# HGRN scan of a hybrid trunk step: half-width score levels, summed before the output product, with the finest levels scaled on GpSimd

## The reference

```
b = jnp.cumsum(logf.astype(jnp.float32), axis=2)
causal = jnp.tril(jnp.ones((C, C), dtype=bool))[:, :, None, None]
diff = b[:, :, :, None] - b[:, :, None, :]
decay = jnp.exp(jnp.where(causal, diff, -jnp.inf))
attn = jnp.einsum('bnthk,bnshk,bntshk->bnhts', q, k, decay)
o_intra = jnp.einsum('bnhts,bnshv->bnthv', attn, v)
b_last = b[:, :, -1]
ds = jnp.einsum('bnshk,bnshv->bnhkv', k * jnp.exp(b_last[:, :, None] - b), v)
...
return S * dec[..., None] + dS, S
...
o_inter = jnp.einsum('bnthk,bnhkv->bnthv', q * jnp.exp(b), jnp.moveaxis(S_start, 0, 1))
return (o_intra + o_inter).reshape(B, T, H, V), S_fin
```

## Time and profile before

| | |
|---|---|
| median of 3 runs | 3807.51 us (3803.77 to 3820.35) |
| profiled execution, its own time | 3803.54 us |
| its span | 3801.8 us |
| PE busy | 3068.4 us (81%) |
| DVE busy | 1796.5 us (47%) |
| ACT busy | 764.6 us (20%) |
| POOL busy | 809.9 us (21%) |
| 386 to 419 us: PE, DVE, ACT, POOL busy | 29.53, 24.94, 10.08, 0.00 of 33.00 us |
| granted clock of PE from 352 to 616 us | 1.00 |

### The profile page before, as it was taken

The page is one execution under the profiler, slowest core; times in us unless marked ns, Lnnn a source line. Parts: engine busy times, 40 slices in busy tenths (PEclk is TensorE's granted clock), DMA queues, the critical chain, the costliest instruction groups (busy, mean ns, idle before and its releaser), DMA issues. The chain is left out here.

```text
span 3801.8 us, 41834 instructions
## 1 busy us (share of the span) xinstructions
PE 3068.4 (81%) x15224; PEld 1731.3 (46%) x15224; DVE 1796.5 (47%) x3832; ACT 764.6 (20%) x1538; POOL 809.9 (21%) x812
## 2 busy tenths in 40 slices
PE   8698886689699999979987776777777777777776
PEld 2475775247476666747543323233323333333332
DVE  0004776424444333333145676556566655664443
ACT  0202223100322121221021212112212121221212
POOL 0000000000000001000014443444444443443442
PEclk9899999699799999989998888888888888988888
DMA  6211000111010110115149998999999999999996
GB/s 268 96 43 43 20 20 12 54 59 58 26 38 29 38 37 29 38 44 193 50 161 356 380 377 327 389 379 375 365 394 382 379 371 383 382 382 378 375 376 252
DMA packets 123662, 794.63 MB, mean 209 GB/s; under 512 B 15127, under 2 KB 16919, under 8 KB 39032
## 3 DMA queue, kind: packets, MB, share of 16 engines
q0 software_dynamic: 92160, 671.13, 44.7%
q1 hardware_dynamic: 31352, 121.42, 9.0%
HBM read 775.98 MB, written 16.52 MB: 208 GB/s over the span
## 5 line engine op out<-in xcount | busy, mean ns | idle before, releaser
L1997 PE MATMUL pr_psy<-pr_rows,pr_diag 128*128 128x512 f32 x2560 | 1312.0, 673 | 447.9 <-ACT pr_diag L2052 447.6
L1997 PEld LDWEIGHTS pr_psy<-pr_rows,pr_diag 128*128 128x128 f32 x2560 | 541.5, 217 | 1215.4 <-issue 665.3
L2179 DVE CUSTOM_DVE_ANT_0 pr_rows<-pr_rows,pr_h_tok 128x1024 f32<-128x1024 f32 x640 | 779.6, 1226 | 647.2 <-DMA pr_rows<-in_p_uv,pr_now 644.9
L1935 POOL DMA_INDIRECT pr_rows<-in_p_uv,pr_now x640 | 727.7, 1137 | 1031.2 <-PE pr_psy L1997 909.0
L1547 POOL TENSOR_TENSOR yT<-rw_sys,rw_bmask 128x128 f32<-128x128 f32 x40 | 18.1, 454 | 1543.6 <-DVE rw_sys L1646 1543.6
L2047 ACT ACTIVATE pr_act<-pr_dot 128x4 f32<-128x4 f32 x160 | 32.8, 205 | 1326.8 <-DVEq L2183 1326.8
L1291 PE MATMUL rw_gate_ps<-hT,rw_gate_w 128*128 128x320 f32 x768 | 262.8, 461 | 3.2 <-ACT rw_gate L1485 3.2
L2052 ACT ACTIVATE pr_diag<-con,pr_weight 128x128 f32<-128x128 f32 x640 | 204.6, 390 | 58.2 <-DVE pr_weight L2189 57.4
L1291 PEld LDWEIGHTS rw_gate_ps<-hT,rw_gate_w 128*128 128x128 f32 x768 | 129.4, 190 | 55.1 <-issue 14.4
L287 PE MATMUL hg_ps<-hT,hg_w 128*128 128x320 f32 x512 | 139.9, 437 | 16.4 <-DMA hg_w<-in_w_in 16.4
L287 PE MATMUL rw_ps<-hT,rw_w 128*128 128x320 f32 x480 | 131.5, 438 | 12.7 <-DMA rw_w<-in_w_in 12.7
(11 more groups left out here) (372 smaller groups left out, 3255.7 us busy)
## 6 DMA issues: line engine op xcount, KB each, us to landing
ada_w<-in_w_ada SPq DMA_DIRECT2D x8, 3072.0 KB, 10.5
rw_gate_w<-in_w_in SPq DMA_DIRECT2D x24, 512.0 KB, 4.1
pr_rows<-in_p_uv,pr_now POOLq DMA_INDIRECT x640, 9.3
hg_w<-in_w_in SPq DMA_DIRECT2D x16, 512.0 KB, 3.4
rw_w<-in_w_in SPq DMA_DIRECT2D x15, 512.0 KB, 3.5
gate_scratch<-rw_gate SPq DMA_DIRECT2D x24, 320.0 KB, 4.2
mg_gate<-gate_scratch SPq DMA_DIRECT2D x24, 320.0 KB, 3.3
mg_wb<-in_w_branch SPq DMA_DIRECT2D x24, 256.0 KB, 2.7
```

Source lines behind the costliest of these rows:

```text
L1935: nc.gpsimd.indirect_dma_start(out=rows[:, r].rearrange("p u d -> p (u d)"), out_offset=None, in_=A["p_uv"], in_offset=bass.IndirectOffset ...
L1997: last = nc.tensor.matmul(ps_y[:, c % 2, a], diag[:, r], rows[:, r, 1, a * 512:(a + 1) * 512], start=(first and r == 0), stop=False, skip_ ...
L2179: nc.vector.tensor_tensor_reduce(out=rows[:, r, 0], in0=rows[:, r, 0], in1=h_tok[:, c], scale=1.0, scalar=0.0, op0=ALU.mult, op1=ALU.add, ...
```

## The change

Levels 1 to 6 and the diagonal only connect positions of the same half of a chunk (64 positions). Their products are now done for each half alone, into the two halves of the partitions, so that each takes 64 columns of a PSUM bank. Level 0 connects one half with the other, and takes 64 columns as well (`FAR`). The eight arrays of a step, 1024 columns before, are 512 now (`HG_W`). VectorE multiplies them with a mask of that form, waits for itself, and sums the seven arrays of the halves into `near` with one reduce. The output then needs one product for each half (`near`), one for `FAR`, and the product with the state in two halves.

The scaling of levels 4 to 6 and of the two end arrays is now done by GpSimd in a list of its own, after `exp_done` of the second exponential; its last instruction raises `x_ready`. VectorE keeps levels 0 to 3, spread over steps 3 and 4, and raises `scaled`. TensorE waits for both before the transposes. `ps_s` and `ps_o` share one tensor of four banks.

```diff
--- before.py
+++ after.py
@@ -37,6 +37,9 @@
 GN_EPS = 64e-5
 LEVELS = [64, 32, 16, 8, 4, 2, 1]
 NL = len(LEVELS)
+H64 = [slice(0, HD), slice(HD, P)]
+HG_W = (NL + 1) * HD
+FAR = slice(NL * HD, HG_W)
 
 
 PARAMS = [("b_ada", 48), ("norm1", 8), ("norm2", 8), ("final", 8), ("lb", 8), ("hgrn_norm", 1),
@@ -365,20 +368,21 @@
                         nc.vector.tensor_copy(i_tok[:, c], ps_i[:, c % 2]).then_inc(i_taken, 1)
 
         NE = NL + 2
-        mask = sb("mask", [P, 2, NL + 1, P])
+        mask = sb("mask", [P, 2, HG_W])
         reset = sb("reset", [P, RESET_W])
         lf = sb("lf", [P, RESET_W])
         cum = sb("cum", [P, RESET_W])
         kT = sb("k", [P, 2, NCH, P])
         E = sb("E", [P, 2, NE, NCH, P])
         dec = sb("dec", [P, 2, NCH])
-        att = sb("att", [P, 2, NL + 1, P])
+        att = sb("att", [P, 2, HG_W])
+        near = sb("near", [P, 2, HD])
         khat = sb("khat", [P, 2, NCH, P])
         S = sb("S", [P, 3, DK])
         S_in = sb("S_in", [P, 8, DK])
-        ps_s = ctx.enter_context(nc.psum_tensor("hg_pss", [P, 2, NL + 1, P], F32))
+        ps_so = ctx.enter_context(nc.psum_tensor("hg_pss", [P, 4, 512], F32))
+        ps_s, ps_o = ps_so[:, 0:2], ps_so[:, 2:4, 0:HD]
         ps_t = ctx.enter_context(nc.psum_tensor("hg_pst", [P, 1024], F32))
-        ps_o = ctx.enter_context(nc.psum_tensor("hg_pso", [P, 512], F32))
 
         ps_d = ps_t[:, 6 * P:7 * P]
         ps_y = ctx.enter_context(nc.psum_tensor("hg_psy", [P, 512], F32))
...
@@ -397,6 +402,19 @@
 
 
         steps = [(g, g // 4, g % 4, c) for g in range(8) for c in order(g // 4)]
+        POOL_FROM = 4
+
+        def scale_level(eng, g, v):
+
+            d, h, b, w = g // 4, g % 4, g % 2, LEVELS[v]
+            q = qT[:, h].rearrange("p (c t) -> p c t", t=P)
+            lo, hi = (kT[:, b], q) if d == 0 else (q, kT[:, b])
+            x = E[:, b, v].rearrange("p c (n t) -> p c n t", t=2 * w)
+            for src, s in ((lo, slice(0, w)), (hi, slice(w, 2 * w))):
+                y = src.rearrange("p c (n t) -> p c n t", t=2 * w)[:, :, :, s]
+                ins = eng.tensor_tensor(x[:, :, :, s], x[:, :, :, s], y, ALU.mult)
+            return ins
+
         with nc.Block() as block:
             @block.sync
             def _(sp):
@@ -448,6 +466,17 @@
                 for n in range(18, 20):
                     take_hyena(n)
 
+            @block.gpsimd
+            def _(pool):
+                for g in range(8):
+                    pool.wait_ge(exp_done, 2 * g + 2)
+                    q = qT[:, g % 4].rearrange("p (c t) -> p c t", t=P)
+                    for v in range(POOL_FROM, NL):
+                        scale_level(nc.gpsimd, g, v)
+                    for n, x in ((NL, q), (NL + 1, kT[:, g % 2])):
+                        ins = nc.gpsimd.tensor_tensor(E[:, g % 2, n], E[:, g % 2, n], x, ALU.mult)
+                    ins.then_inc(x_ready, 1)
+
             @block.tensor
             def _(pe):
                 def hyena(n, first, end):
@@ -474,6 +503,7 @@
                     b = g % 2
                     if n % NCH == 0:
                         pe.wait_ge(x_ready, g + 1)
+                        pe.wait_ge(scaled, g + 1)
                         if g >= 1:
                             pe.wait_ge(khat_ready, g)
                         for cc in range(NCH):
@@ -481,9 +511,13 @@
                         last.then_inc(tr_done, 1)
                     if n >= 2:
                         pe.wait_ge(att_ready, n - 1)
-                    for v in range(NL):
-                        nc.tensor.matmul(ps_s[:, n % 2, v], E[:, b, v, c], E[:, b, v, c], start=True, stop=True)
-                    nc.tensor.matmul(ps_s[:, n % 2, NL], kT[:, b, c], qT[:, h, c * P:(c + 1) * P],
+                    q = qT[:, h, c * P:(c + 1) * P]
+                    for v in range(1, NL + 1):
+                        lhs, rhs = (E[:, b, v, c], E[:, b, v, c]) if v < NL else (kT[:, b, c], q)
+                        for half in H64:
+                            nc.tensor.matmul(ps_s[half, n % 2, (v - 1) * HD:v * HD], lhs[:, half], rhs[:, half],
+                                             start=True, stop=True)
+                    nc.tensor.matmul(ps_s[:, n % 2, FAR], E[:, b, 0, c], E[:, b, 0, c, H64[1 - d]],
                                      start=True, stop=True).then_inc(s_done, 1)
 
                 def outputs(n):
@@ -505,9 +539,9 @@
                     if n >= 1:
                         pe.wait_ge(o_taken, n)
                     first = n % NCH == 0
-                    for v in range(NL + 1):
-                        last = nc.tensor.matmul(ps_o[:, 0:P], iv, att[:, n % 2, v], start=(v == 0),
-                                                stop=(v == NL and first))
+                    for i, half in enumerate(H64):
+                        nc.tensor.matmul(ps_o[:, i], iv[half], near[half, n % 2], start=True, stop=first and i == d)
+                    last = nc.tensor.matmul(ps_o[:, 1 - d], iv, att[:, n % 2, FAR], start=False, stop=first)
                     if not first:
                         k = n % NCH
                         if k == 1:
@@ -516,7 +550,8 @@
                         else:
                             pe.wait_ge(st_ready, 4 * g + k)
                             src = S[:, 1 + k % 2]
-                        last = nc.tensor.matmul(ps_o[:, 0:P], src, E[:, b, NL, c], start=False, stop=True)
+                        for i, half in enumerate(H64):
+                            last = nc.tensor.matmul(ps_o[:, i], src, E[:, b, NL, c, half], start=False, stop=True)
                     last.then_inc(o_done, 1)
 
                 for n in range(4):
...
@@ -583,29 +616,24 @@
                             nc.vector.tensor_tensor(E[:, b, NL + 1], exc, zero, ALU.subtract).then_inc(dec_sub, 1)
 
                     def scale(v):
-                        w = LEVELS[v]
-                        dve.wait_ge(exp_done, 2 * g + (1 if v < 4 else 2))
-                        x = E[:, b, v].rearrange("p c (n t) -> p c n t", t=2 * w)
-                        for src, s in ((lo, slice(0, w)), (hi, slice(w, 2 * w))):
-                            y = src.rearrange("p c (n t) -> p c n t", t=2 * w)[:, :, :, s]
-                            nc.vector.tensor_tensor(x[:, :, :, s], x[:, :, :, s], y, ALU.mult)
-
-                    def scale_ends():
-                        nc.vector.tensor_tensor(E[:, b, NL], E[:, b, NL], q, ALU.mult)
-                        nc.vector.tensor_tensor(E[:, b, NL + 1], E[:, b, NL + 1], kT[:, b], ALU.mult).then_inc(
-                            x_ready, 1)
+                        dve.wait_ge(exp_done, 2 * g + 1)
+                        ins = scale_level(nc.vector, g, v)
+                        if v == POOL_FROM - 1:
+                            ins.then_inc(scaled, 1)
 
                     return [[gates], [sums] + [lambda v=v: level(v) for v in range(4)],
                             [lambda v=v: level(v) for v in range(4, NL)] + [to_ends],
-                            [lambda v=v: scale(v) for v in range(4)],
-                            [lambda v=v: scale(v) for v in range(4, NL)] + [scale_ends]]
+                            [lambda v=v: scale(v) for v in range(2)],
+                            [lambda v=v: scale(v) for v in range(2, POOL_FROM)]]
 
                 def chunk(n, meanwhile):
                     g, d, h, c = steps[n]
                     dve.wait_ge(s_done, n + 1)
                     if n >= 2:
                         dve.wait_ge(o_done, n - 1)
-                    nc.vector.tensor_tensor(att[:, n % 2], ps_s[:, n % 2], mask[:, d], ALU.mult).then_inc(att_ready, 1)
+                    link(nc.vector.tensor_tensor(att[:, n % 2], ps_s[:, n % 2], mask[:, d], ALU.mult))
+                    nc.vector.tensor_reduce(near[:, n % 2], att[:, n % 2, 0:NL * HD].rearrange("p (v t) -> p t v", t=HD),
+                                            AX, ALU.add).then_inc(att_ready, 1)
                     k = n % NCH
                     if k != NCH - 1:
                         dve.wait_ge(ds_done, 4 * g + k + 1)
@@ -627,11 +655,11 @@
                     for step in meanwhile:
                         step()
                     dve.wait_ge(o_done, n + 1)
-                    o = K.yT[0][:, h, c * P:(c + 1) * P]
+                    o = K.yT[0][:, h, c * P:(c + 1) * P].rearrange("p (i t) -> p i t", i=2)
                     if d == 0:
-                        nc.vector.tensor_copy(o, ps_o[:, 0:P]).then_inc(o_taken, 1)
+                        nc.vector.tensor_copy(o, ps_o).then_inc(o_taken, 1)
                     else:
-                        nc.vector.tensor_tensor(o, o, ps_o[:, 0:P], ALU.add).then_inc(o_taken, 1)
+                        nc.vector.tensor_tensor(o, o, ps_o, ALU.add).then_inc(o_taken, 1)
 
                 for steps_of in prepare(0):
                     for step in steps_of:
...
@@ -2295,12 +2322,15 @@
         con[:, CCOL["tneg"] + 1 + c] = -tl[c * P:(c + 1) * P]
```

(13 more changed lines are left out.)

## The result

The changed kernel took 3838.4 us (median of six runs, 3831.2 to 3841.6) and the one before, on the same chip, 3814.9 us (3803.8 to 3824.6). The ratio is 1.0059, 95% interval 1.0039 to 1.0078: slower by 23.5 us between the medians and by 22.5 us by the ratio, where +23.0 was predicted. (The predicted time itself, about 3831, came from an earlier median of 3807.5 for the kernel before, 7 us lower than here.) The profiled execution of the changed kernel took 3837.5 us, its span 3835.7 us. Medians of the kernel before moved between 3814.0 and 3817.1 over the four sets of runs here. A length read from the traces leaves out what the other stages do, and I use two.

The account below looks back on a forecast made before the run. A ring of waits through TensorE, VectorE and ScalarE was taken to bound the HGRN scan's rounds 0 to 6. Seven handovers at +3.9 us (+27.3) and round 7 (-4.3) gave +23.0 on 3807.5: about 3831 us, range 3808 to 3847.

Parts of the forecast that it names:

- L518's records: Sign in the new profile: TensorE's half products of the scores would stand 0.043 us apart.
- To the end of the second exp: From a round's start: 26.28 less 2 x 0.23 (scores) and 0.59 (wait), plus 2 x 0.15 (mask product and sum): 25.5 us.
- GpSimd's chain: Eight GpSimd instructions between second exp and transposes: 8.05 us, plus 1.9 while VectorE's products with two SBUF inputs block them.
- The clock: TensorE idles 5.2 us, or 7.1 with blocking, before the transposes, so each round starts at half clock: +1.8 us.
- Round 7: Last round, nothing prepared: scores and outputs save 6.1 us; with the start at half clock, -4.3.
- Sum: Round 33.55 + 1.9 + 1.8 = 37.25 us; seven handovers +27.3, last round -4.3: +23.0 us in total.
- B: Rival: either GpSimd's blocking or the clock's fall doesn't come: 3817 us; with neither, 3803. Chance 0.25.
- C: Rival: strided access is dear; reduce at its upper bound 3838 us, short-run GpSimd instructions at 1.2 us 3847. Chance 0.15.
- E: Rival: TensorE's column halves don't run side by side, 1.9 us a score step: 3837 us. Chance 0.07.
- D: Rival: GpSimd's work is shorter than VectorE's own second half and the clock stays: 3770 us. Chance 0.05.
- A: The prediction's own case, its full sum: 3831 us, own range 3819 to 3843. Chance 0.48.
- the ring: HGRN scan's chain from transposes through scores, Hyena, gates, scan, second exp and products to the next transposes, 33.34 us before.

Follow-up runs that it names:

- e8: e3 with masked levels written column by column, so the sum reads neighbours: sum 0.93 to 0.62 us, mask product 0.68 to 1.03; ratio 1.0021.
- e1: Changed kernel without VectorE's scaling of levels 2 and 3 (outputs not the layer's): GpSimd chain 8.75 us instead of 9.75; ratio 1.0070.
- e2: Changed kernel with 20 extra, unused TensorE products in its wait at the start of rounds 1 to 7: mean round 35.84 us, ratio 1.0055.
- e9: Kernel before with only the move of scaling to GpSimd, scores, mask and outputs as they were: mean round 37.52 us, ratio 1.0094.
- e3: Changed kernel with all products back on VectorE in their old places, so only compact scores, sum and shorter outputs: mean round 35.83 us, ratio 1.0037.
- e12: e4 with gates before the state-copy wait, six step-0 Hyena matmuls behind the outputs, and VectorE adding three levels to three others: round 33.87 us, ratio 1.0010.
- e4: e3 without VectorE's sum; TensorE accumulates the seven masked levels in halves: mean round 30.96 us, ratio 0.9968.

## Why the prediction was right

Its mechanism held, and its sum fell right partly by luck, since sizes in it were off both ways. What held: the round at 37.49 (37.25 predicted), the transposes released by GpSimd, seven waits of 5.6 us on average and 6.3 at most, GpSimd instructions of over 1 us, half clock at the start of rounds 1 to 7. One sign did not: L518's records are 0.031 apart, not 0.043. Among the matmuls' own waits the one for GpSimd is the largest, as predicted; by the weight loads the wait for `near` is as long (40.7 us, in 21 pieces). By its steps, for the round shown:

- **To the end of the second exp**: 27.3 with the clock's 1.8 predicted, 454.19 - 427.05 = 27.14 measured. In the first round, at the full clock, it was 25.53 where the sum without the clock gave 25.5. Inside it two sizes were off and cancelled, twice each: that is luck. A score step is 1.24 at full clock, not 1.55: 24 half records take 0.75 us, 0.031 each, so the two column halves run side by side, near the lower bound of 1.1. The pair is 1.56, not 1.28; the sum at 0.93 lies between the bounds of 0.62 and 1.09, and e8 showed that the stride is the reason.
- **GpSimd's chain**: 9.95 predicted (8.05 + 1.9), 9.75 measured. Nearly unblocked it is 8.75 (e1), as the six instructions with short runs go at 0.96 and not 0.82, while the two of 640 take 1.52 (1.50 predicted). That the short runs are the reason was not tested by itself. Blocking adds 1.0, not 1.9. So two errors of nearly 1 us cancelled here too, again by luck. The prediction let GpSimd stand still for all of VectorE's instruction. In fact each waits for the other: VectorE's products show 1.28 us instead of 0.48, as they wait about 0.8 us for GpSimd's to end, and GpSimd loses only about 0.25 at each meeting. The Trainium skill, "SBUF — State Buffer", section SBUF: two separate sides, says so (the one that starts first keeps the shared ports for its whole instruction), and the trace agrees in both directions.
- **The clock**: 1.8 predicted, 1.65 by e2's mean round; to the exp's end it is 1.6 to 2.1 and once 4.2 (27.1 to 27.6 and 29.7 against 25.5). That it comes back after 3.9 us of work held (3.6). TensorE's wait before it is 5.5 us and not 7.1: step 4's mask product began 1.4 us behind the exp (455.61 - 454.19), not 0.3, and TensorE's last products with it. The fall came all the same. The dip in mid-round was missed.
- **Round 7**: -4.3 predicted. From its first transpose to the end it took 30.06 us before (585.75 to 615.81) and 25.90 now (613.66 to 639.56): -4.2. The parts hold too, since in e9 it is 31.70 (613.52 to 645.22): +1.6 for the half clock (1.8 predicted), -5.8 for the compact part (-6.1).
- **Sum**: +23.0 predicted, +23.5 by the medians, +22.5 by the ratio and +24.3 by the stage's length. Seven rounds give 7 x 4.15 = 29.0, and from the last copy to the end it is 24.5 instead of 29.3, -4.7.

Of the rivals, B is ruled out by e1 and e2, which show both additions. C is half true: strided access costs, but between its bounds (0.93 of 0.62 to 1.09 for the sum, 0.96 of 0.82 to 1.2 for GpSimd's). E is wrong, and D too. The time alone, 3838.4, would fit C's first case (3838) and E (3837); the difference to the kernel before, +23.5, and the rows speak for A.

What the prediction did not see is what the compact scores do to the clock. The 0.75 us that it let them gain up to the exp's end came as forecast at the full clock. But alone they lose 2.5 us a round (e3), 0.1 of it at the full clock (33.44 against 33.34) and 2.4 because TensorE, with less work and longer waits, loses its clock. The move to GpSimd alone costs 2.6 us at the full clock (26.23 + 9.64 = 35.87 against 33.3) and 1.7 through the clock. That is why the two losses, 2.5 and 4.2, don't add: the changed kernel pays 2.2 us at the full clock (25.53 + 10.03 = 35.56, where the prediction had 33.55 + 1.9 = 35.45) and 1.9 through the clock, once.

## What to carry to other kernels

Ask of each edit whether its instructions are in the ring or beside it. Seven levels accumulated by TensorE in idle room cost the round nothing that shows, their sum on VectorE did, and the version without the sum and without GpSimd is ahead of both kernels (0.9968, interval 0.9944 to 0.9991; 17 us of the stage). A wait that closes when you serve it is not yet a gain: look for the next instruction on that engine that hangs on the other's order, and count what still stands ahead of it. And before taking work off TensorE, look at how long it would then stand idle, because the clock is part of the price.

## What the runs showed of the hardware that I had not expected

- The granted clock fell in e3 though no wait of the matmuls was longer than 2.8 us, and in e12 during the second of two waits of 1.61 and 1.96 us. In the kernel before, waits of 1.45 and 1.60 us at the same places left it at 1.00. What decides between them these runs don't show.
- Two column halves of the array run side by side in fp32: 24 records of 128x64 in 0.75 us (437.27 to 438.02), 0.031 each, where the prediction's estimate for one after the other, from rows 3, was 0.055. The row halves of the outputs take (455.59 - 453.88) / 28 = 0.061 each in e4.
- GpSimd and VectorE block each other whole instructions at a time, but the loss is uneven: 0.8 us for VectorE (1.28 instead of 0.48), 0.25 for GpSimd (1.25 instead of 0.99) at each meeting.
